# A two-layer decoder step: twelve tiles of the first projection move from its end into the stage of cached values

## The reference, cut to what matters

```python
gate_b, gate_c, u, q, k, v = jnp.split(h @ w_in, split_at, axis=-1)
conv_out, new_hist = causal_dwconv(gate_c * u, conv_hist, conv_w)
y_a = gate_b * conv_out
y_b = attend(q, k, v)          # prompt: 256 rows; sample: 8 sequences x 4 rows
y = jnp.concatenate([y_a, y_b], axis=-1) @ w_out
```

## Time and profile before

| what | us |
|---|---|
| median of 3 runs (lowest, highest) | 1102.64 (1100.86, 1103.34) |
| span of the profiled execution | 1097.7 |
| PE busy in it | 1031.3 (94%) |
| DVE busy | 705.6 (64%) |
| ACT busy | 503.3 (46%) |
| POOL busy | 52.9 (5%) |
| HBM read, written | 192.59 MB, 12.17 MB |

### The profile page before, as it was taken

How to read it: one execution, slowest core, us unless ns; L and a number is a source line. 1 busy time by engine, 2 the same in 40 slices (tenths; PEclk the granted TensorE clock), 3 DMA queues, 4 the chain that set the end, 5 groups by cost and what they waited for, 6 DMA issues and landing times.

```text
span 1097.7 us, 21745 instructions
## 1 busy us (share of the span) xinstructions
PE 1031.3 (94%) x8763; PEld 947.1 (86%) x8763; DVE 705.6 (64%) x1296; ACT 503.3 (46%) x902; POOL 52.9 (5%) x97
## 2 busy tenths in 40 slices
PE   8999999888889999999889999889999799999996
PEld 7988888533579999999889999768889799999995
DVE  5644678655448566643498997778984676566343
ACT  5222444232355344343458675554764543444341
POOL 8001300000000000000000000021000000000000
PEclk9999999879898999999989999899999899999998
DMA  9637999999953555455524555089135265554501
GB/s 303 185 99 251 331 348 348 339 348 348 338 173 115 161 180 160 150 168 166 171 78 153 170 177 154 1 281 330 45 121 157 81 189 154 176 169 135 182 30 43
DMA packets 193074, 206.17 MB, mean 188 GB/s; under 512 B 7172, under 2 KB 185561, under 8 KB 192923
## 3 DMA queue, kind: packets, MB, share of 16 engines
q1 hardware_dynamic: 174046, 178.65, 51.6%
q10 hardware_dynamic: 15232, 14.68, 4.2%
q0 software_dynamic: 3696, 11.45, 3.3%
HBM read 192.59 MB, written 12.17 MB: 187 GB/s over the span
## 4 chain that ended last, share of the span: by engine, by line
PE 84%; DVE 7%; DMA 3%; ACT 2%; POOL 1%; issue 1%; SPq 1%; ACTq 0%; POOLq 0%; DVEq 0%
PE acc L822 21%; PE acc L824 21%; PE acc L823 21%; PE trb L915 3%; PE scb L936 3%; PE acc L915 3%; PE scb L1048 2%; PE scb L793 1%; DVE RR L1802 1%; DMA ring<-in_state_ssm_dram 1%; DMA ring<-in_cache_v_dram 1%; SPq L597 1%; DVE X L2211 1%; DVE Y L2210 1%; PE acc L1196 1%
## 5 line engine op out<-in xcount | busy, mean ns | idle before, releaser
L822 PE MATMUL acc<-HX,WHL 128*128 128x288 f32 x928 | 281.0, 303 | 14.8 <-DVE HX L1814 10.2
L823 PE MATMUL acc<-HX,WHL 128*128 128x288 f32 x928 | 277.5, 299 | 0.0
L824 PE MATMUL acc<-HX,WHL 128*128 128x288 f32 x928 | 277.1, 299 | 0.0
L1401 ACT ACTIVATE WHL<-ring 128x1024 fp32r<-128x1024 f32 (+1 forms) x140 | 138.8, 1039 | 200.3 <-PE acc L824 200.3
L1825 DVE TENSOR_TENSOR WHL<-ring,WHL 128x1024 fp32r<-128x1024 f32 (+1 forms) x140 | 163.5, 1208 | 69.5 <-ACT WHL L1401 69.4
L822 PEld LDWEIGHTS acc<-HX,WHL 128*128 128x128 f32 x928 | 178.4, 192 | 18.2 <-issue 12.9
L823 PEld LDWEIGHTS acc<-HX,WHL 128*128 128x128 f32 x928 | 179.9, 194 | 0.2
L824 PEld LDWEIGHTS acc<-HX,WHL 128*128 128x128 f32 x928 | 179.4, 193 | 0.0
L1401 ACT ACTIVATE W<-ring 128x1024 fp32r<-128x1024 f32 x84 | 82.6, 1031 | 130.4 <-PE acc L824 130.4
L1825 DVE TENSOR_TENSOR W<-ring,W 128x1024 fp32r<-128x1024 f32 x84 | 97.1, 1197 | 54.1 <-ACT W L1401 54.1
L822 PE MATMUL acc<-HX,W 128*128 128x288 f32 x352 | 105.7, 300 | 5.5 <-DVE HX L1814 5.1
(11 more groups left out here) (413 smaller groups left out, 1855.3 us busy)
## 6 DMA issues: line engine op xcount, KB each, us to landing
ring<-in_l_w_in_dram SPq DMA_DIRECT2D x32, 1024.0 KB, 5.4
ring<-in_l_ffn_gate_dram SPq DMA_DIRECT2D x22, 1024.0 KB, 5.3
ring<-in_l_ffn_up_dram SPq DMA_DIRECT2D x22, 1024.0 KB, 5.3
ring<-in_l_ffn_down_dram SPq DMA_DIRECT2D x16, 1024.0 KB, 5.1
Z<-in_cache_k_dram SPq DMA_DIRECT2D x52, 256.0 KB, 7.7
ring<-in_cache_k_dram SPq DMA_DIRECT2D x52, 256.0 KB, 7.3
Z<-in_cache_v_dram SPq DMA_DIRECT2D x48, 256.0 KB, 7.1
ring<-in_cache_v_dram SPq DMA_DIRECT2D x48, 256.0 KB, 6.6
```

What stands on the lines that cost most here:

```text
L822: pe.matmul(out, w[:, 0, at:at + P], part_at(k, 0), start=(k == 0), stop=False)
L823: pe.matmul(out, w[:, 0, at:at + P], part_at(k, 1), start=False, stop=False)
L824: last = pe.matmul(out, w[:, 1, at:at + P], part_at(k, 0), start=False, stop=(k == kdim - 1))
L1401: act.activation(split_weights(i)[:, 0, half], ring[:, slot_of(u), half], ACT.Copy).then_inc(w_hi, 1)
```

## The change

The projection now ends after the twelve tiles of q, k and v (M_QKV = 12). The twelve tiles of the convolution are projected between the cached values: `conv_tile(0)` before them, `conv_tile(2b+1)` in the middle of `values(b)` and `conv_tile(2b+2)` behind it, in the order gate_c, u, gate_b. Their six weight units are loaded from POOLq into one buffer WST, each when the low parts of both tiles of the unit before have been made; `high_parts(j)` on ACT and `low_parts(j)` on DVE split one tile at a time into WC[j % 2].

The cached keys and values go through one POOL of six slots, one in Z and five in `ring`: slot p (0 to 31 keys, 32 to 63 values) is loaded when slot p - 6 has been used. The first six wait only for the ring slots that the projection's six units leave. HIST_POS goes from 7 to 4. Small buffers that lay over HX0 move, since HX0 is now read to the end of `conv_tile(11)`; KOUT lies under the second half of the new weights, so the first `high_parts` waits for the stores of keys and values. On DVE the computation of the convolution moves from b = 1 to 5 to b = 3 to 6, and on ACT `prompt_step(0)` moves behind `copy_output(0)`.

```diff
-    in0_units = column_units(l0_w_in, MQ * P, (M_IN0 - MQ) // 2) + column_units(l0_w_in, 0, MQ // 2)
+    M_QKV = M_IN0 - MQ
+    in0_units = column_units(l0_w_in, MQ * P, M_QKV // 2)
+    CONV_TILES = list(range(CA, MQ)) + list(range(CA))
+    N_CONV = len(CONV_TILES)
+    conv_units = column_units(l0_w_in, CA * P, CA) + column_units(l0_w_in, 0, CA // 2)
...
-    HIST_POS = 7
+    HIST_POS = 4
...
+        WST = a.take(KD, UC)
+        in_z = a.take(H, J4, DH)
+        in_ring = Area(ring[:, :, :].rearrange("p r n -> p (r n)")).take(R, H, J4, DH)
+        POOL = [in_z] + [in_ring[:, i, :, :, :] for i in list(range(1, R)) + [0]]
+        NPL = len(POOL)
...
-                        if slot < KVS:
-                            sp.wait_ge(v_used, (NB - 1) * KVS + slot + 1)
-                        else:
-                            sp.wait_ge(*lo[last_in0(slot)][1])
+                        sp.wait_ge(v_used, last_in_ring(slot) - N_SLOT + 1)
...
+                    if p == 0:
+                        sp.wait_ge(tr_full, TR_PAR)
+                    elif p < NPL:
+                        sp.wait_ge(*lo[last_in0(p % R)][1])
+                    elif p < N_SLOT + NPL:
+                        sp.wait_ge(tr_full, TR_K + J4 * (p - NPL + 1))
+                    else:
+                        sp.wait_ge(v_used, p - NPL - N_SLOT + 1)
...
@@ gpsimd, behind the stores of the new keys and values
+            for i, (src, _) in enumerate(conv_units):
+                if i:
+                    pool.wait_ge(cw_lo, 2 * i)
+                pool.dma_start(WST, src).then_inc(cw_in, 16)
...
@@ tensor
+            def conv_tile(j):
+                pe.wait_ge(cw_lo, j + 1)
+                bank, w = acc_open(), WC[j % 2]
+                for k in range(KD):
+                    at = slice(k * P, (k + 1) * P)
+                    pe.matmul(bank[:, 0:NT], w[:, 0, at], HX0[:, k, 0, :], start=(k == 0), stop=False)
+                    pe.matmul(bank[:, 0:NT], w[:, 0, at], HX0[:, k, 1, :], start=False, stop=False)
+                    last = pe.matmul(bank[:, 0:NT], w[:, 1, at], HX0[:, k, 0, :], start=False, stop=(k == KD - 1))
+                last.then_inc(acc_full, 1)
...
                     if j == J4 - 1:
                         last.then_inc(v_used, 1)
+                        if s == 1 and 2 * b + 1 < N_CONV:
+                            conv_tile(2 * b + 1)
...
                           start=False, stop=True).then_inc(o_full, 1)
+                if 2 * b + 2 < N_CONV:
+                    conv_tile(2 * b + 2)
...
+            conv_tile(0)
             turn_sample(0)
...
@@ scalar
+            def high_parts(j):
+                act.wait_ge(cw_in, 16 * (j // 2 + 1))
+                if j >= 2:
+                    act.wait_ge(acc_full, marks["conv", j - 2])
+                act.activation(WC[j % 2][:, 0, :].rearrange("p (k n) -> p k n", n=P), WST[:, :, j % 2 * P:(j % 2 + 1) * P],
+                               ACT.Copy).then_inc(cw_hi, 1)
...
+                if p == N_SLOT - 4:
+                    act.wait_ge(kv_stored, marks["kv_stored"])
+                    high_parts(0)
...
+                for s in range(1, KVS, 2):
+                    p = N_SLOT + b * KVS + s
+                    if p + NPL < 2 * N_SLOT:
+                        act.wait_ge(v_used, b * KVS + s + 1)
+                        load(p + NPL)
+                    if 2 * b + 2 + s // 2 < N_CONV:
+                        high_parts(2 * b + 2 + s // 2)
+                copy_output(b)
...
@@ vector
+            def low_parts(j):
+                dve.wait_ge(cw_hi, j + 1)
+                w = [WC[j % 2][:, i, :].rearrange("p (k n) -> p k n", n=P) for i in range(2)]
+                dve.tensor_tensor(w[1], WST[:, :, j % 2 * P:(j % 2 + 1) * P], w[0], ALU.subtract).then_inc(cw_lo, 1)
+            def conv_output(j):
+                free(dve.tensor_tensor(BIG[:, CONV_TILES[j], :], take()[:, 0:NT], RR[:, :], ALU.mult))
...
+                    low_parts(0)
             own_probabilities(0)
             move_scores(NB - 1)
+            conv_output(0)
+            low_parts(1)
...
+            conv_output(1)
+            low_parts(2)
+            conv_output(2)
+            low_parts(3)
             query_max(1)
...
+                for j in (2 * b + 1, 2 * b + 2):
+                    if b and j < N_CONV:
+                        conv_output(j)
+                        if j + 1 < N_CONV:
+                            low_parts(j + 1)
```

More of the change, by code:

```diff
@@ L134, in hybrid_decoder_kernel @@
         X = sb("X", [P, KD, NT])
+        with nc.sbuf_tensor("WCY", [P, 2, KD * P], F32R) as t:
+            WCY = t
         Y = sb("Y", [P, KD, NT])
@@ L276, in hybrid_decoder_kernel @@
         ext = sb("ext", [P, 2, EXT])
-        co_s = sb("co_s", [P, CC, 3 + 3 * NB])
+        late = sb("late", [P, CC * (3 + 3 * NB) + NT + 3 * P + CX * (NB + 1) + 2 * NP])
+        a = Area(late)
+        co_s = a.take(CC, 3 + 3 * NB)
+        hs = a.take(NT)
+        tc = a.take(3, P)
+        dec = a.take(CX, NB + 1)
+        YTMP = a.take(2, NP)
+        a = Area(late)
+        SM = a.take(15, NB * NBLK // 2)
+        CUP = a.take(CA, NP + 2)
+        CUS = a.take(CA, NB, T + 2)
+        POWN = a.take(NB * QT)
         wdt = sb("wdt", [P, KD, SH])
         hp3 = sb("hp3", [SH, 3])
-        hs = sb("hs", [P, NT])
-        tc = sb("tc", [P, 3, P])
-        dec = sb("dec", [P, CX, NB + 1])
         decin = sb("decin", [SH, NB + 1])
@@ L317, in hybrid_decoder_kernel @@
         w_used = sem("w_used")
-        kv_in = [sem(f"kv_in{i}") for i in range(KVS)]
-        kv2_in = [sem(f"kv2_in{i}") for i in range(KVS)]
+        kv_in = [sem(f"kv_in{i}") for i in range(NPL)]
+        cw_in = sem("cw_in")
+        cw_hi = sem("cw_hi")
+        cw_lo = sem("cw_lo")
         v_used = sem("v_used")
@@ L509, in hybrid_decoder_kernel @@
         done, used, unit_of = [], 0, []
-        for first, tiles, kparts in ((0, M_IN0, 1), (ACC_OUT0, KD, 1), (ACC_GU0, 2 * FM, 1), (ACC_DOWN0, KD, -(-FM // KD)),
+        for first, tiles, kparts in ((0, M_QKV, 1), (ACC_OUT0, KD, 1), (ACC_GU0, 2 * FM, 1), (ACC_DOWN0, KD, -(-FM // KD)),
                                      (ACC_IN1, 2 * DT_POS, 1), (ACC_DT + 1, CC + CX - 2 * DT_POS, 1),
@@ L587, in last_in0, with last_in_ring, load_sequence @@
                 return max(u for u in range(len(units_a)) if slot_of(u) == slot)
-            def load_sequence(cache, b, wait, order=range(KVS)):
+            def last_in_ring(slot):
+                return max(p for p in range(2 * N_SLOT) if p % NPL and (p % NPL) % R == slot)
+            def load_sequence(cache, b):
                 page = page_numbers(nc.sync.engine, b, 0, NPAGES)
-                for s in order:
-                    wait(s)
+                for s in range(KVS):
+                    p = b * KVS + s + (0 if cache is cache_k else N_SLOT)
+                    if p == 0:
[6 more added lines that the diff above has]
+                        sp.wait_ge(v_used, p - NPL - N_SLOT + 1)
                     for g in range(J4):
-                        if (b < 2 or g != ACT_K) if cache is cache_k else (s, g) not in ACT_PAGES:
-                            dst, src, arrived = load_page(cache, b, page[J4 * s + g], s, g)
-                            sp.dma_start(dst, src).then_inc(arrived, 16)
+                        if (p < NPL or g != ACT_K) if cache is cache_k else (s, g) not in ACT_PAGES:
+                            dst, src, landed = load_page(cache, p, page[J4 * s + g], g)
+                            sp.dma_start(dst, src).then_inc(landed, 16)
             sp.dma_start(pages[:, :], page_table.rearrange("b n -> (b n)").unsqueeze(0)).then_inc(ld_pages, 16)
@@ L607, in _ @@
             load_units(R, len(units_a))
[L608 to L616, removed]
+            for cache in (cache_k, cache_v):
+                for b in range(NB):
+                    load_sequence(cache, b)
             load_units(len(units_a), len(units))
@@ L1484, in _ @@
                     sample_exp(3)
+            act.wait_ge(kt_used, 2 + N_SLOT - 1)
+            high_parts(1)
             def prompt_exp(h):
@@ L1536, in _ @@
                         sample_exp(later)
-                for s in range(1, KVS, 2):
-                    if b + 2 < NB:
-                        act.wait_ge(v_used, b * KVS + s + 1)
-                        load_values(b + 2, s)
-                copy_output(b)
             copy_transposed(TR_COA, coT_a[0:2 + 2 * NB, 0:2 * P], trb[0][0:2 + 2 * NB, 0:2 * P])
@@ L1550, in tile @@
                 def tile(k):
-                    return Y[:, k, :] if input_norm else acc[(first_acc + k) % 4][:, 0:NT]
+                    return Y[:, k, :] if input_norm else acc_bank(first_acc + k)[:, 0:NT]
                 def gain(k):
@@ L1852, in _ @@
             input_norm(0, (0,))
-            for i, m in enumerate(list(range(MQ, M_IN0)) + list(range(MQ))):
+            for i, m in enumerate(range(MQ, M_IN0)):
                 bank = take()
```

103 lines of the change are left out of this document (50 added, 53 removed).

## The result

The change made the kernel slower: 1106.22 us median of 11 executions (1101.33 to 1112.39) against 1100.88 of 11 of the kernel before on the same chip (1096.06 to 1103.34). The ratio is 1.0050, 95% interval 1.0028 to 1.0071. The forecast was 1094.0, faster, with 1105 as the upper end of its range: wrong in sign and outside the range. The profiled executions differ in the same way, 1103.0 against 1097.7 of span. The 4.9 us that were put around the span of the kernel before are too much: every execution whose time and span are both on record takes 1.7 to 2.0 us more than its span (here 1104.75 against 1103.0). So the profiled execution of the kernel before was a quick one, some 1099.4 by that estimate.

What follows compares the result with a forecast made beforehand. Bytes were taken to bound the values, PE nearly everything else, leaving PE a 16.4 us hole to fill. 41.7 won in the projection less 33.1 lost in the values gives 8.6: 1102.6 to 1094.0, range 1081 to 1105.

Steps and rivals of the forecast that it cites:

- Part 1: Projection: without the convolution's tiles it ends earlier, a gain of 41.7 us; the keys begin at 64.5 in place of 106.2.
- the histories: Projection, at pair 4: copying and transposing them was put at 2.7 us, bounds 2.3 and 6.3.
- Part 2: Keys stage: six slots suffice, no stall taken (bound 2 us); the keys end at 161.7.
- Part 3: Values stage with twelve tiles: 16.2 us a sequence, paced by the one buffer WST; stage grows from 89.9 to 123.0.
- L: Issue and landing of a weight unit's load from POOLq into WST: 8 us taken, 9.2 for unit 1.
- nothing is added there: End of the values stage, up to the output projection: 24.4 us as before, so it starts at 284.7.
- A new one of 2 can stand there: Values stage: PE waits 2 us for sum_exponentials(1), behind low_parts(7) on DVE, covered by the loader's slack.
- The start: Start of values: unit 1 lands at 175.9, split by 178.4; PE waits 3 us, tile 2 ends at 182.5.
- The loader becomes the bound, slower: Rival, values stage: one transfer at a time, landing held up by V pages or DVE; 1105 to 1116, chance 0.16.
- It comes out even: Rival, values stage: L = 9.2 with half-slow or slow tiles, 18.0 to 19.3 a sequence; 1100 to 1105, chance 0.12.

Runs made afterwards that it cites:

- late unit 0: The changed kernel with the load of unit 0 held until the keys of slot 21 have been turned: 1105.64 us, ratio 1.0061.
- small units: The changed kernel with units 1 to 5 loading one of their eight blocks (128 KB in place of 1 MB): 1095.05 us, ratio 0.9945.
- the sum moved: The changed kernel with sum_exponentials(1) on DVE ahead of the tiles' evictions and low parts of b = 2: 1102.03 us, ratio 1.0018.
- three orders: The changed kernel with, on DVE, convolution ahead of sample_output, sum_exponentials(1) ahead of the low parts, low_parts(1) ahead of move_scores(7): 1093.29 us, ratio 0.9941.
- unit 1 earlier: The changed kernel with low_parts(1) on DVE ahead of move_scores(7) and conv_output(0): 1103.13 us, ratio 1.0023.
- fourth order: Changed kernel with three DVE orders edited, plus turn_max(1) and prompt_step(0) ahead of tile 2 on PE, their DVE steps around low_parts(2): 1089.37 us, ratio 0.9902.
- the repeat: The changed kernel itself run again, unedited, against the kernel before: 1106.55 us, ratio 1.0043.

## Why the prediction was wrong

**Part 1 was right.** The 12th eviction came at 59.49 and the keys at 64.65, with the histories at 3.7 in place of 2.7, inside their bounds.

**Part 2, "I take no stall (bound: 2 us)"**, was off by 1.6, inside the bound. 2.3 of waits for cached keys stand there, where the kernel before has none. The late unit 0 shows that the unit's megabyte makes one of them; the shares of the stores and of the six slots were not taken apart.

**Part 3, the loader**, was nearly right in its numbers: L at 7.1 for 8, and 16.6 a sequence for 16.2 ((254.80 - 205.06) / 3). The pace hangs on other things, though. With small units the sequences take as long; with the sum moved, one takes 15.0 with all the bytes. Where the prediction let the loader's loop set the pace, PE did, by its own work and one wait of 1.95 with a lower clock: the three sequences took 15.1, 19.9 and 14.7, and that their mean is near 16.2 is luck. The Trainium skill, "SBUF — State Buffer" (SBUF: two separate sides), has a load from GpSimd stand still while DVE runs an operation in its two-port mode. No run here shows such a load: with DVE busy for half of the stage, the four units inside the loop landed in 5.8 to 7.5. Unit 1 (9.42) and unit 0 (11.1) took longer than 9.2; what held them is not shown.

**The steps that failed** are three. The first two are on DVE's queue; the third is the loader's start, which DVE's order makes longer:

1. "From the same point (268.9) to the output projection (293.3) before it was 24.4, and nothing is added there." 31.3 stand there, the largest miss, 6.9. The diff puts the last tap and the gate at b = 6; the prediction took the tail over from the kernel before without laying DVE's new list against it. Two waits stand there for it, 3.27 and 0.9 more of the prompt's, and the clock is 0.84 over this stretch, 0.91 in the kernel before. Undone, it gives back 1 to 5 us, 3 against the mean of the unedited traces (33.1 to 30.1).
2. "A new one of 2 can stand there [...]; it lies in the loader's slack." The wait was 1.95, as said, but the loader had next to no part in the pace (0.24 of waits between tiles 2 and 10), so nothing covered it, and the clock behind it doubled its price in most executions: undone, tile 6 to 8 goes from 19.9 (16.9 to 20.1 over seven traces) to 15.0 (14.7 to 16.4 over three). The two other sequences were quicker than the 16.2 forecast, so the net miss over all three is only 1.1.
3. The start. A wait of 3 with "part of it at the low clock" was 4.6, with 14 slow matmuls. L was taken as 9.2 here and came at 9.42, but the low parts were ready at 180.7, not 178.4: 1.7 of this is the keys' late end, while PE was ready at 176.1, only 0.7 after the forecast. With small units the wait is 0.9, with `low_parts(1)` first 2.6. Counted from the keys' end this step is off by 1.5: the low parts are 0.6 later, and tile 2 is 0.9 slower. Tile 2 to tile 4, with the prompt's wait of 3.5, missed by as much again.

The three undone together give 1093.3, beside the 1094.0 that was forecast. That the figure is so near owes something to chance: it has terms that were off on both sides (the keys, the histories, the pace, and 4 us behind the output projection in that execution). It also starts from 1102.64, a median of three; 8.6 below the 1100.88 of eleven is 1092.3.

Of the rivals, none was right. "The loader becomes the bound, slower" had the sign and, but for the start, the wrong mechanism. "It comes out even" named a cause that mattered, the clock after gaps of about 2 us, but hung it on the loader. Its argument that the clock fell after each such gap holds in the kernel before; in other traces it stayed full behind 2.60 and 2.87. A rival "DVE's order holds PE up", with the three places read off the diff, was missing; its price could have been had from the rows: the earlier trace rows show that PE waits for DVE's small steps for 7.6 us in the stage already, and the new tiles set 1.7 us of DVE's work in front of each.

**Left open:** the part from the output projection on took 802 to 812 us in executions with the same work there, so that single spans don't resolve 5 us; why the run with small units gains some 4 us more than its stage shows; and whether the waits for low parts in the fastest version would go with a second WST, which was not tried.

## What to carry to other kernels

Work that is put into an engine's idle time fills only the idle time that has the wait's cause elsewhere. Here PE's hole of 16.4 us was in part made by short steps on DVE, and each moved tile brought 1.7 us of DVE's work with it; put in front of those steps, it made new holes as large as the ones it filled. So lay out the new order of every engine that the moved work touches, not only of the one that it is moved for, and ask at each step who waits for the small thing behind the large one. And price a wait of TensorE with the clock behind it: here 2 us cost between 2 and 5.

## What the runs showed of the hardware

- Behind a wait of 1.95 us TensorE ran at 1.2 GHz in place of 2.4 for the next 8 us in one execution; behind the same wait (1.94) at the same place it stayed at full clock in another of the same code. Over seven executions with this wait the stretch took 16.9 to 20.1 us. Behind 2.66 before tile 2 the clock fell (three orders), behind 2.60 and 2.87 it did not (unit 1 earlier, fourth order), and the last of these kept a granted clock of 1.00 over the whole stage.
- At 349 to 351 GB/s TensorE was busy for 14.7 to 14.8 of 15.0 us. The same work at 304 GB/s and full clock kept it busy for 15.06 (the repeat), so the higher traffic did not slow it.
- A load of 1 MB from POOLq, beside SPq and ACTq in stages at 295 and 334 GB/s, landed after 5.8 to 11.1 us, 7.1 at the median; with five of the six units cut to an eighth the median was still 4.6.
